# Stick-breaking attention with its first head's weights transposed one pair later, and one more projection tile ahead of the first transposes in memory attention

## The reference, cut to what matters

```
# stick-breaking attention: 8 heads of 64 columns, for each block of 128 queries
z = einsum('bhtd,bhsd->bhts', q, k) * scale
log_fail  = where(strict, log_sigmoid(-z), 0)
log_after = cumsum(log_fail, axis=3, reverse=True) - log_fail
w = where(strict, exp(log_sigmoid(z) + log_after), 0)
y_sb = einsum('bhts,bhsd->bhtd', w, v)

# memory cross-attention: 4 heads of 128 columns on 256 memory rows
scores = einsum('bhsd,bhmd->bhsm', rmsnorm(q), rmsnorm(k)) * scale
y_xa = einsum('bhsm,bhmd->bhsd', softmax(scores), v)

# after both: merged = sum over branches of sigmoid(gate_b) * (y_b @ w_out_b)
```

## Time and profile before

| | |
|---|---|
| median of the runs | 2009.96 us |
| the profiled execution, its own time | 2010.26 us |
| its span, first to last instruction | 2008.5 us |
| PE busy | 1982.9 us, 99% of the span |
| DVE busy | 1451.0 us, 72% |
| ACT busy | 603.3 us, 30% |
| POOL busy | 348.9 us, 17% |
| mean granted TensorE clock | 0.998 |

### The profile page before, as it was taken

The page is one execution under the profiler, slowest core; times in us unless marked ns, Lnnn a source line. Parts: engine busy times, 40 slices in busy tenths (PEclk is TensorE's granted clock), DMA queues, the critical chain, the costliest instruction groups (busy, mean ns, idle before and its releaser), DMA issues.

```text
span 2008.5 us, 31639 instructions
## 1 busy us (share of the span) xinstructions
PE 1982.9 (99%) x12854; PEld 1595.8 (79%) x12854; DVE 1451.0 (72%) x2209; ACT 603.3 (30%) x1045; POOL 348.9 (17%) x317
## 2 busy tenths in 40 slices
PE   9999999999999999999999999999999999999999
PEld 7888888887777777778888877777888888888887
DVE  6666766667876777767998887676666779859973
ACT  2000122222555545423884234574310010000000
POOL 2112111111101011011111212111122212222221
PEclk9999999999999999999999999999999999999999
DMA  5333322322212122222222433221233333333332
GB/s 183 96 93 105 90 83 91 88 91 64 94 57 64 54 68 72 65 64 84 65 74 84 123 94 88 65 63 55 73 94 95 105 94 99 101 95 94 95 100 89
DMA packets 53361, 173.38 MB, mean 86 GB/s; under 512 B 6464, under 2 KB 6720, under 8 KB 53088
## 3 DMA queue, kind: packets, MB, share of 16 engines
q1 hardware_dynamic: 48112, 161.33, 26.5%
q10 hardware_dynamic: 5104, 10.03, 1.8%
HBM read 169.17 MB, written 2.16 MB: 85 GB/s over the span
## 4 chain that ended last, share of the span: by engine, by line
PE 84%; DVE 10%; ACT 3%; issue 2%; DMA 1%; ACTq 0%; DVEq 0%; SPq 0%
PE ps_lin L1935 24%; PE ps_lin L1937 23%; PE ps_lin L1936 23%; PE ps_att L1984 6%; PE ps_aux L1984 4%; DVE arena L439 3%; ACT arena L1350 2%; DVE arena L433 2%; PE ps_att L1993 2%; DVE w_lo L433 1%; DVE arena L436 1%; ACT L1356 1%; PE ps_lin L1955 1%; DVE y_lo L433 0%; PE ps_lin L1957 0%
## 5 line engine op out<-in xcount | busy, mean ns | idle before, releaser
L1935 PE MATMUL ps_lin<-xw_hi,w_hi 128*128 128x512 f32 x1704 | 689.8, 405 | 0.8 <-DVE w_lo L433 0.5
L1937 PE MATMUL ps_lin<-xw_hi,w_lo 128*128 128x512 f32 x1704 | 665.8, 391 | 0.0
L1936 PE MATMUL ps_lin<-xw_lo,w_hi 128*128 128x512 f32 x1704 | 664.9, 390 | 0.0
L415 POOL TENSOR_SCALAR w_hi<-raw 128x1024 fp32r<-128x1024 f32 (+2 forms) x309 | 345.0, 1117 | 1641.5 <-PE ps_lin L1937 1522.2
L1350 ACT ACTIVATE arena<-arena 128x512 f32<-128x512 f32 (+7 forms) x328 | 202.1, 622 | 713.1 <-DVE arena L433 323.6
L433 DVE TENSOR_TENSOR w_lo<-raw,w_hi 128x1024 fp32r<-128x1024 f32 (+2 forms) x340 | 378.2, 1115 | 45.4 <-POOL w_hi L415 17.5
L1937 PEld LDWEIGHTS ps_lin<-xw_hi,w_lo 128*128 128x128 f32 x1704 | 320.3, 188 | 68.6
L1935 PEld LDWEIGHTS ps_lin<-xw_hi,w_hi 128*128 128x128 f32 x1704 | 320.8, 188 | 67.5 <-issue 3.5
L1936 PEld LDWEIGHTS ps_lin<-xw_lo,w_hi 128*128 128x128 f32 x1704 | 321.2, 189 | 58.5
L433 DVE TENSOR_TENSOR arena<-ps_lin,rstd 128x512 f32<-128x512 f32 (+3 forms) x220 | 147.7, 671 | 193.5 <-PE ps_lin L1937 185.2
L1935 PE MATMUL ps_lin<-y_hi,w_hi 128*128 128x512 f32 (+1 forms) x544 | 205.3, 377 | 0.0
(11 more groups left out here) (188 smaller groups left out, 1676.0 us busy)
## 6 DMA issues: line engine op xcount, KB each, us to landing
raw<-in_w_up SPq DMA_DIRECT2D x44, 512.0 KB, 3.6
raw<-in_conv_w_in SPq DMA_DIRECT2D x32, 512.0 KB, 3.6
raw<-in_fox_w_in SPq DMA_DIRECT2D x32, 512.0 KB, 3.6
raw<-in_gdn_w_in SPq DMA_DIRECT2D x32, 512.0 KB, 3.6
raw<-in_w_gate SPq DMA_DIRECT2D x24, 512.0 KB, 3.6
raw<-in_swa_w_in SPq DMA_DIRECT2D x20, 512.0 KB, 3.7
raw<-in_w_ml SPq DMA_DIRECT2D x16, 512.0 KB, 3.7
raw<-in_w_down SPq DMA_DIRECT2D x16, 512.0 KB, 3.6
```

The source lines that it names most:

```text
L415: pool.tensor_scalar(w_whole(n, kc * c)[0], w_raw(n, kc * c), 1.0, 0.0, mult, add).then_inc(s("w_rounded"), 1)
L1935: pe.matmul(o, wh, hi, start=first and k == 0, stop=False)
L1936: pe.matmul(o, wh, lo, start=False, stop=False)
L1937: ins = pe.matmul(o, wl, hi, start=False, stop=last and k == kc - 1)
```

## The change

Three edits go together. On PE the ten transposes of head 0 no longer stand in pair 0's third tile; they stand behind the scores of pair 1, three pieces ahead of those of head 1. On ACT the three copies of head 0's transposes move from behind the exponential of head 0 to behind the logarithms of head 2. And in memory attention the first head has two tiles between its scores and its transposes, where it had one, so that every later head's transposes and products come one tile later in the stream; the last stretch of the stream is one tile shorter. The numbers of matmuls, of DVE's and of ACT's instructions stay as they are, but the waits of pair 1's scores for copies of pair 0's transposes go, since those transposes come later now.

```diff
                 sb_logs(2 * j)
+                if j == 1:
+                    sb_turned(0)
                 if j:
                     sb_turned(2 * j - 1)
                 if last:
                     xa_square(0)
                 sb_logs(2 * j + 1)
                 sb_weights(2 * j)
+                if 0 < j and not last:
+                    sb_turned(2 * j)
                 if not last:
-                    sb_turned(2 * j)
                     sb_weights(2 * j + 1)
...
-                        if j and i > 1 and (i, half) != (3, 0):
+                        if j > 1 and i > 1 and (i, half) != (3, 0):
                             pe.wait_ge(s("sb_PT"), 3 * (2 * j - 2) + (1 if i == 3 else 2 + half))
...
                     sb_scores(j)
                     sb_turn(j)
                     tile()
+                    if j == 1:
+                        sb_weights(0, 1)
+                        project(3)
                     sb_weights(2 * j - 1, j)
...
-                if j < SB_H // 2 - 1:
-                    sb_last_tile(2 * j, 5 if j else 6)
+                if 0 < j < SB_H // 2 - 1:
+                    sb_last_tile(2 * j, 5)
+                elif j == 0:
+                    tile()
...
-                tile(2 if h else 1)
+                tile(2)
...
-            tile(4 * ND)
+            tile(4 * ND - 1)
```

## The result

The changed kernel takes 2021.82 us (median of four runs, 2021.69 to 2022.35) against 2010.39 us of the kernel before (four runs, 2009.28 to 2011.34). The ratio is 1.0055, with a 95% interval of 1.0042 to 1.0068: slower by 11.4 us, where the forecast was 8.6 us. The span of the profiled execution is 2020.0 us, 11.5 more than before. PE's busy time is 1986.5 us, 3.6 more with the same matmuls, which is a first sign of a lower clock; the rest is idle time.

The account below looks back on a forecast made before the run. PE bounds the kernel, busy 1982.9 of 2008.5 us. The terms 1.23 + 0.8 + 3.0 - 2.33 + 4.3 + 0.9 + 0.7 give +8.6 us on 2009.96, so 2018.5 us; 8-in-10 range 2012.5 to 2021.5.

Parts of the forecast that it names:

- the summed case: Whole kernel: all terms of both parts added, +8.6 us, 2018.5 us; chance 0.50, its own range 2016.5 to 2019.5.
- the rival with a second fall: Memory attention: the clock also falls behind one of its waits, at 3.0 us more, 2021.5 us; chance 0.10.
- The wait in stick-breaking: Pair 1's last two scores: PE idles 3.7 to 4.5 us for ACT's copies, in place of 2.25 us.
- The ten transposes still owed: Stick-breaking: head 0's transposes, formerly between the wait and the scores, now come after a longer wait; +1.23 us.
- the collision with the scans: Stick-breaking: POOL's `w_hi` falls upon the start of head 1's scans on DVE and lengthens them; +0.8 us, bounds 0 and 0.81.
- The clock: Behind the new wait in stick-breaking PE's clock falls to about half for some 6 us; +3.0 us, bounds 0 and 3.0.
- the rival that the clock stays up: Stick-breaking: no fall of the clock behind the new wait; 2015.5 us, or 2014.7 without the collision; chance 0.17.
- The term of -2.33: Memory attention, first head: the wait ahead of its transposes goes, since 5.42 us of gate tile g1 precede them; -2.33 us.
- the four waits for low parts: Memory attention: PE waits for DVE's split gate weights, 2.15 us at heads 1 and 2 (+4.3), then +0.9 and +0.7 us.
- These waits are as short as those that left the clock at 1.00: Memory attention: no fall of the clock behind the waits for low parts, as behind earlier stretches of 2.40 and 2.49 us.
- The rivals with a gain: Memory attention gains (2012.7 us, chance 0.10), stick-breaking alone gains (2011.3, 0.06), or both gain (2005.4, 0.07).

Follow-up runs that it names:

- the rounding held back: The whole change, with POOL holding the one rounding that fell upon head 1's scans until DVE has subtracted; 2020.60 us, ratio 1.0044 to the kernel before.
- five fillers: The whole change plus five matmuls without use on PE ahead of the wait for the copies of pair 1's scores; 2019.30 us, ratio 1.0038 to the kernel before.
- the early low part: Memory attention's edits alone on the kernel before, plus one line: DVE writes the next gate weight's low part before waiting for the head's product; 2007.38 us, ratio 0.9982.
- the roundings held: Memory attention's edits alone on the kernel before, with POOL holding g4's and g6's roundings until DVE wrote g3's and g5's low parts; 2015.68 us, ratio 1.0018.
- the memory half: The kernel before with only the change's two lines in memory attention, stick-breaking left as it was; 2017.06 us, ratio 1.0033.
- the run with seven fillers: The whole change plus seven matmuls without use on PE ahead of the wait for the copies of pair 1's scores; 2020.61 us, ratio 1.0051 to the kernel before.

## Why the prediction was right, point by point

The direction, the two mechanisms and their places were right; the sum was 2.8 us short. Stick-breaking cost less than summed (4.3 us, not 5.0) and memory attention up to its last product more (6.3 us, not 2.9): one collision was left out there, 0.7 us at each of two heads, and the clock fell at one more place, for 1.6 us.

The result is near the edge of the forecast. The measured 2021.82 us lie 0.3 above the upper end of the range, 2021.5; 11.4 us above the 2009.96 from which the forecast started is 2021.4, just inside. The narrower range of the summed case, up to 2019.5, was missed. That the time comes so near to the 2021.5 of the rival with a second fall is in part luck: the second fall cost 1.6 us and not 3.0, the first 0.9 less than summed, and the collision and small differences filled the gap.

- **The wait in stick-breaking.** Forecast 4.5 us at the last two scores, released by ACT's copies; it is 4.45. Changing ACT's order alone moved it, which shows that the place in ACT's program was the cause.
- **The ten transposes still owed** (+1.23) **and the collision with the scans** (+0.8). Scans of 3.76 us against 2.97 with the rounding held back show the second; the last scores then came 0.8 us sooner behind pair 1's first ones. Together with the clock's 2.1 us the two make 4.1 of the 4.3 us measured.
- **The clock.** It fell where it was forecast, and the rival that the clock stays up falls. Forecast price 3.0, measured 2.1: the stretch behind the wait was 5.50 us at 0.50, not 6.08 at 0.51, and by the prediction's own formula that is 2.75. Nor does half the clock cost quite half of the stretch: the matmuls of a piece start 0.43 us apart in it and 0.23 us behind it, and the two last scores take 1.12 us until the next transposes at the full clock (five fillers) and 1.64 in the change, half a microsecond more.
- **Memory attention.** The term of -2.33 came, as did the four waits for low parts; the early low part shows their cause. The forecast of 2.15 us each at heads 1 and 2 was too small: the heads took 3.06 and 4.66 us longer. Of the 3.06, 0.7 is the low part's 1.94 us in place of 1.23. **This term was mis-sized:** the start of the low part stayed as far behind the product as forecast (7.96 us, and 7.97 in the earlier trace rows), but its 1.23 us were taken from the earlier trace rows, where nothing on POOL ran beside it; in the new order the end of the branch tile, just ahead of it, releases a rounding on POOL that falls upon it. Holding that rounding back gave 1.23 us again. What is left of the 3.06 above the forecast, some 0.2 us, is not explained: each of these heads loses 0.3 us more than the wait that the trace lists (3.06 and 2.73, with the roundings held 2.33 and 2.02). It is the same collision that the prediction had priced in the other half. The Trainium skill's rule of the exclusive port (SBUF — State Buffer, section on SBUF's two separate sides) would have given a collision here too. The runs agree that VectorE is held up, by 0.7 to 0.8 us a time; POOL's rounding was longer as well, 1.45 and 1.25 us, where it took 1.05 when it was held back.
- "These waits are as short as those that left the clock at 1.00" was the other miss. Behind the second wait of 2.73 us the window shows 0.62, and head 2 took 1.6 us more than head 1. The rival of a second fall, given a chance of 0.10, is what happened in this execution, at a lower price than its 3.0.

The rivals with a gain fell as the prediction argued: DVE's subtraction of head 1 did not come earlier; counted from the value transposes of pair 0, it came 0.8 us later.

## What to carry to other kernels

When a wait on the busiest engine is removed by moving its work back, look up what that engine meets next and where this stands in the helper's program: here both next things stood behind waits of their own, and the gain turned into a loss. The cure was on the helpers, not on the busy engine: one line that let VectorE write a weight where it was idle turned the memory half's 6 us lost into 3.7 us won (2017.06 and 2007.38 us against 2011.11 us of the kernel before on that chip). And when the order on the busy engine changes, follow what its finished pieces release on the other engines, for that falls upon new neighbours.

## What the runs showed of the hardware that was not expected

Whether the clock falls behind an idle stretch of PE did not go by the stretch's length alone. In the twelve profiled executions it fell behind all three waits of 3.66 to 4.45 us in stick-breaking and behind the only one of 2.64 us. Of the waits for ACT's `sq`, 2.90 to 2.93 us long, which every kernel here has at the place of the first two windows in the earlier trace rows, it fell behind nine of twelve; of those of 2.73 us, behind three of ten; of 2.33 us, two of four; of 2.24 and 2.25 us, none of four; of 2.01 and 2.02 us, one of two. So even the wait from which the prediction took its price left the granted clock at 1.00 in three executions, and equal waits in one execution differed (1.00 behind the first 2.73 us of the changed kernel, 0.62 behind the second).

Where two otherwise equal stretches could be laid side by side, the price was 1.6 us (head 2 against head 1 of the changed kernel, 26.23 - 24.63), 2.1 us (with and without the five fillers) and 2.8 us (head 1 against head 2 in the run with seven fillers, 27.43 - 24.61). In the last the clock stayed low for longer behind the wait:

```profile
1420.46:1426.50 6.04, 6.04 (x14) 4.83 (x15) 3.25 (x5) 1.91 (x2) 0.00 (x0) 0.50 0.38 128
```

So a wait of 2 to 3 us carries a cost that one profiled execution may not show.
